# Attention output kept transposed into the mixing stage, with the norm gains moved into w_o and a fourth PSUM bank for turned scores

## The chip, the core and the metric

The kernel is one program on one core of a Trainium2 chip. The metric is device time in microseconds (us) of a run, the median of several. Work is spread over five engines that each run their own instruction stream in order: PE (TensorE: matrix products and transposes), DVE (VectorE), ACT (ScalarE), POOL (GpSimd) and SP (SyncE, which issues DMAs). They meet only at semaphores. A wait written in an engine's stream holds everything that is queued behind it on that engine.

## The reference, cut to what matters

One layer of an encoder runs on 2048 prompt rows and 64 sample rows (2112 rows), model width 1024. All arithmetic is float32.

```python
h = rms_norm(x, g_pre_mix)
q, k, v, logf, gate_b, cu = project(h, w_in, b_f)
o_attn = attn_fn(q, k, v, logf).reshape(b, t, ATTN_DIM)      # 8 heads x 64
o_conv = gate_b * short_conv(cu)                              # 512 channels
merged = jnp.concatenate([rms_norm(o_attn, g_attn_out), rms_norm(o_conv, g_conv_out)], axis=-1)
x = x + rms_norm(merged @ w_o, g_post_mix)
h2 = rms_norm(x, g_pre_mlp)
m = jnp.square(jax.nn.relu(h2 @ w_up)) @ w_down
x = x + rms_norm(m, g_post_mlp)
```

The attention of the sample rows also reads a cache of 512 past keys. `g_attn_out` and `g_conv_out` are gains per channel, so they can stand on either side of the product with `w_o`.

## The kernel before, in words

There are four stages, one after the other: the input projection (`project_inputs`, to about 636 us of the profile), attention (`attend`, to about 1093 us), mixing (`mix_rows`, to about 1310 us) and the MLP (`mlp`). Every float32 product is made from rounded high parts and low rests, as hi\*hi + hi\*lo + lo\*hi, so each operand is split into two parts beforehand.

**Attention.** `attention_order` (L1095) writes one list of steps for two heads, and every engine walks that list four times, each taking the steps that concern it. `queue_of` (L1075) only moves some kinds of step a few places later on ACT and DVE (`DELAY`, L1072). The kinds are: S, a piece of scores (PE L1471 to L1475, DVE L1434); M, the row maximum and the exponentials (DVE L1440, ACT L1389); T, turning a block of exponentials onto its side through PE (L1484, bank `t_bank`) and splitting it (ACT `p_hi` L1393, DVE `p_lo` L1446); V, the product with the values (PE L1500, L1501, bank `o_bank`); O, ACT's copy of the finished `o_bank` to SBUF (`o_t`, L1398); N, the rest of a group; L, the loads of the next head's operands on SP.

A head has five groups of query rows, worked in the order g0 (rows 0 to 511), g4 (the 64 sample rows), g1, g2, g3; their T steps number 4, 2, 8, 12, 16. In `o_t` the 128 partitions hold two halves of 64, one from the high part of the values and one from the rest, that must still be added. N does that in the kernel before: PE turns the four 128x128 blocks into `n_bank` (L1507), ACT copies them (`o_n`, L1404), POOL adds the halves (L1349) and multiplies by the reciprocal of the row sums (L1352), and SP stores the rows to the DRAM tensor `attn` (L1302). N of a group stands after the first two T steps of the group that follows. `att` has five buffers.

L stands at the start of each head. Between the two heads of one list it comes ahead of the N of the first head's g3 (`L ... T T N(g3)`); where the list wraps round, the N of the second head's g3 is the last step of the list and so comes ahead of L. It issues ten DMAs (L93 to L107, about 6 MB), or the eight loads of `w_o` (L1581) in the last head. All of them are issued by SP, which also issues the stores of N.

During the last head POOL splits the eight row blocks of `w_o` into `w_hi` and `w_lo` (`split_weights`, L1599; which blocks after which N is `SPLITS`, L1067), and prepares tile 0 of the mixing stage (L1614 to L1643).

**Mixing.** `mix_rows` works on 17 tiles of rows; tile 0 is the 64 sample rows. For a tile, DVE multiplies the attention rows by the gain (`ag`, L1880), PE turns them (`turn`, L1961), ACT and DVE split them (`a_hi` L1795, `a_lo` L1884); the conv output already lies transposed, and POOL squares and sums it over blocks (L1754 to L1760), multiplies the gain (`cg`, L1763) and makes the rest (`c_lo`, L1766), with `c_hi` from ACT (L1789). The sum of squares over channels is taken by ACT for the attention rows (L1785) and by PE for the conv part (`sum_squares`, L1969), one tile ahead of the products. PE then makes the two products (`multiply`, L1975, banks `a_bank` and `c_bank`, 24 matmuls each). ACT and DVE scale, add, normalise, add x and normalise again (`part` L1822, `mixed` L1900, `scaled` L1908, `x2` L1913, `h2` L1923), and PE turns `h2` (L2025), which ACT copies (L1830). On PE the steady order is: product a of tile t, turn and sum_squares of tile t+1, product c of tile t, turn of h2 of tile t-1. On ACT the front work of tile t+1 begins right behind the copies L1830.

## Time and profile before

| | |
|---|---|
| runs | 2746.72, 2746.88, 2739.39 us; median 2746.72 |
| span of the profiled execution | 2738.8 us |
| own time of the profiled execution | not recorded apart from its span; the median of the runs lies 7.9 us above that span |
| PE busy | 2664.4 us, 97% of the span |
| DVE, ACT, POOL busy | 1520.9, 1126.8, 1308.7 us (56%, 41%, 48%) |
| attention stage | about 636 to 1093 us |
| mixing stage | about 1093 to 1310 us |

The span runs from the first to the last instruction. Busy is the time in which an engine had an instruction in work; PE's ends are modelled, so that its neighbours overlap. In a timeline a line gives the start, the duration, the engine, the source line, the operation and its tiles; "x4" stands for four merged into one. A DMA line on SP gives the time that the issue took on SP, not the transfer.

### The profile page before, as it was taken

How to read it: one execution, taken by the hardware profiler on the slowest of the kernel's cores; microseconds unless marked ns; L12 is line 12 of the kernel's file. 1: busy time of each engine (PE TensorE's matmuls, PEld its weight loads, DVE VectorE, ACT ScalarE, POOL GpSimd, SP SyncE). 2: the span in 40 equal slices, each digit the busy share in tenths (PEclk: the TensorE clock that was granted, in tenths of full speed). 3: DMA queues.
4: the chain of work that ended last, by engine and by line, in shares of the span. 5: the costliest groups of instructions: out<-in, count | busy, mean ns of one | idle time of the engine just before them, and what ended most of it. 6: DMA issues, size and time to landing. Idle time of an engine off the chain costs nothing.

```text
span 2738.8 us, 41595 instructions
## 1 busy us (share of the span) xinstructions
PE 2664.4 (97%) x14966; PEld 2404.3 (88%) x14966; DVE 1520.9 (56%) x2603; ACT 1126.8 (41%) x2099; POOL 1308.7 (48%) x884
## 2 busy tenths in 40 slices
PE   8999999998999999999999999999999999999998
PEld 7899899897887878888899998889999988999996
DVE  5333434247888888666343443665556664556554
ACT  3201301106777877455333332534333344333433
POOL 3233243320110115544476775866556677566664
PEclk9999999999999999999999999999999999999999
DMA  6643544574465543469445456512211272211213
GB/s 196 194 131 102 164 112 138 188 198 123 99 141 132 122 101 113 145 188 252 153 158 176 164 184 218 193 64 74 74 64 61 78 283 94 75 61 63 75 61 108
DMA packets 294353, 364.26 MB, mean 133 GB/s; under 512 B 37576, under 2 KB 245392, under 8 KB 290128
## 3 DMA queue, kind: packets, MB, share of 16 engines
q1 hardware_dynamic: 257152, 316.15, 37.7%
q0 software_dynamic: 11808, 26.74, 3.1%
q10 hardware_dynamic: 25264, 19.66, 2.1%
q8 instruction: 80, 1.31, 0.2%
q14 instruction: 49, 0.40, 0.0%
HBM read 264.30 MB, written 97.94 MB: 132 GB/s over the span
## 4 chain that ended last, share of the span: by engine, by line
PE 45%; POOL 2%; DMA 2%; DVE 1%; issue 1%; ACT 0%; SPq 0%; DVEq 0%; POOLq 0%; ACTq 0%
PE dn_bank L3006 16%; PE up_bank L2982 14%; PE dn_bank L2962 7%; PE up_bank L2937 7%; DMA m_raw_up<-in_w_up 1%; POOL m_y L2517 1%; POOL m_w_up L2466 1%; DMA m_x<-scratch_x 0%; SPq L2342 0%; DVE m_t L2758 0%; DVE m_raw_up L2758 0%; POOL m_u L2509 0%; ACT m_junk L2659 0%; DVE m_y L2863 0%; DVE m_y L2817 0%
## 5 line engine op out<-in xcount | busy, mean ns | idle before, releaser
L3006 PE MATMUL dn_bank<-m_w_dn,m_u 128*128 128x512 f32 x2304 | 528.8, 390 | 0.8 <-DVE m_y L2817 0.5
L3006 PEld LDWEIGHTS dn_bank<-m_w_dn,m_u 128*128 128x128 f32 x2304 | 431.9, 188 | 90.1 <-DVE m_y L2817 0.9
L2982 PE MATMUL up_bank<-m_h,m_w_up 128*128 128x384 f32 x2688 | 476.6, 337 | 9.7 <-DVE m_stage L2772 5.3
L2982 PEld LDWEIGHTS up_bank<-m_h,m_w_up 128*128 128x128 f32 x2688 | 470.6, 189 | 13.7 <-issue 5.8
L2819 DVE TENSOR_TENSOR m_y<-dn_bank,m_y 128x1024 f32<-128x1024 f32 x168 | 205.7, 1224 | 270.4 <-PE dn_bank L3006 270.4
L508 POOL TENSOR_TENSOR w_lo<-w_raw,w_hi 128x1024 fp32r<-128x1024 f32 x72 | 180.9, 2516 | 327.5 <-DVE w_hi L722 327.5
L2509 POOL TENSOR_TENSOR m_u<-m_stage,m_u 128x384 fp32r<-128x384 f32 x128 | 141.5, 1128 | 281.4 <-ACT m_u L2648 281.4
L2466 POOL TENSOR_TENSOR m_w_up<-m_raw_up,m_w_up 128x512 fp32r<-128x512 f32 x128 | 191.8, 1519 | 65.2 <-ACT m_w_up L2616 65.2
L938 PE MATMUL proj<-ha_hi,w_hi 128*128 128x384 f32 (+1 forms) x640 | 212.2, 331 | 0.0
L1446 DVE TENSOR_TENSOR p_lo<-t_bank,p_hi 128x512 fp32r<-128x512 f32 (+1 forms) x336 | 197.9, 599 | 25.2 <-ACT p_hi L1393 24.6
L938 PE MATMUL proj<-ha_hi,w_lo 128*128 128x384 f32 (+1 forms) x640 | 210.0, 328 | 0.0
L938 PE MATMUL proj<-ha_lo,w_hi 128*128 128x384 f32 (+1 forms) x640 | 210.0, 328 | 0.0
L1349 POOL TENSOR_TENSOR att<-o_n 128x256 f32<-128x256 f32 (+1 forms) x40 | 26.2, 654 | 380.1 <-ACT o_n L1404 375.7
L1393 ACT ACTIVATE p_hi<-t_bank 128x512 fp32r<-128x512 f32 (+1 forms) x336 | 171.7, 528 | 65.5 <-PE t_bank L1484 62.5
L2937 PEld LDWEIGHTS up_bank<-m_h,m_up_plain 128*128 128x128 f32 x1440 | 192.4, 188 | 2.5
L2937 PE MATMUL up_bank<-m_h,m_up_plain 128*128 128x256 f32 (+1 forms) x1440 | 193.9, 294 | 0.0
L2648 ACT ACTIVATE m_u<-m_stage 128x384 fp32r<-128x384 f32 x128 | 60.2, 517 | 302.3 <-PE dn_bank L3006 299.6
L2772 DVE TENSOR_TENSOR m_stage<-up_bank,m_stage 128x384 f32<-128x384 f32 x224 | 118.6, 551 | 113.6 <-PE up_bank L2982 107.6
L2616 ACT ACTIVATE m_w_up<-m_raw_up 128x512 fp32r<-128x512 f32 x128 | 76.3, 624 | 242.3 <-PE up_bank L2982 226.4
L2502 POOL TENSOR_TENSOR m_w_dn<-m_raw_dn,m_w_dn 128x2048 fp32r<-128x2048 f32 x32 | 159.4, 4981 | 14.8 <-ACT m_w_dn L2624 14.8
L1500 PE MATMUL o_bank<-p_hi,v_hl 128*128 128x512 f32 (+3 forms) x360 | 139.2, 394 | 8.2 <-DVE p_lo L1446 7.6
L2758 DVE TENSOR_TENSOR m_t<-m_raw_up,m_t 128x512 f32<-128x512 f32 x64 | 145.6, 2276 | 0.0
(304 smaller groups left out, 5674.8 us busy)
## 6 DMA issues: line engine op xcount, KB each, us to landing
m_raw_up<-in_w_up SPq DMA_DIRECT2D x48, 1024.0 KB, 5.4
m_raw_dn<-in_w_down SPq DMA_DIRECT2D x47, 1024.0 KB, 4.9
w_raw<-in_w_in SPq DMA_DIRECT2D x72, 512.0 KB, 4.1
scratch_h_pairs<-m_pieces POOLq DMA_DIRECT2D x12, 1792.0 KB, 8.2
m_h<-scratch_h_pairs SPq DMA_DIRECT2D x14, 1536.0 KB, 11.0
nck<-scratch_ncum SPq DMA_DIRECT2D x8, 1312.0 KB, 18.9
scratch_v_hl<-vhl SPq DMA_DIRECT2D x20, 512.0 KB, 2.7
q_hi<-scratch_q_hi SPq DMA_DIRECT2D x16, 528.0 KB, 7.4
```

What stands on the lines that cost most here:

```text
L508: pool.tensor_tensor(w_lo[:, slot(i)], w_raw[:, i % 2], w_hi[:, slot(i)].bitcast(F32), ALU.subtract).then_inc(w_lo_done, 1)
L938: mm = pe.matmul(out[:, 0:CW[g]], w[:, slot(i), k], h[g][:, k, chunk(g, n)], start=(k == 0 and a == 0), stop=(k == KB - 1 and a == 2))
L1393: act.activation(p_hi[:, x.p, x.cols], t_bank[x.at % T_BANKS][:, x.cols], ACT.Copy).then_inc(hi_done, 1)
L1446: dve.tensor_tensor(p_lo[:, x.p, x.cols], t_bank[x.at % T_BANKS][:, x.cols], p_hi[:, x.p, x.cols].bitcast(F32), ALU.subtract).then_inc(lo_ ...
L2466: pool.tensor_tensor(w_up[:, j, 1], sources[j], w_up[:, j, 0].bitcast(F32), ALU.subtract).then_inc(w_lo_done, 1)
L2502: pool.tensor_tensor(w[:, 1], raw[:, :, :], w[:, 0].bitcast(F32), ALU.subtract).then_inc(dn_lo_done, 1)
L2758: dve.tensor_tensor(to, x, z, op).then_inc(sums_made, 1)
L2819: dve.tensor_tensor(place, bank[:, :], place, ALU.add).then_inc(y_added, 1)
L2937: mm = pe.matmul(up_bank[2 * x + b][:, 0:w], weights[:, b * P:(b + 1) * P], early.rows[2 * x + hp][:, k, :], start=(k == 0 and p == 0), st ...
L2962: mm = pe.matmul(bank[:, cols], u_first[:, x, b, part], w[wp][:, b, cols], start=(b == 0 and p == 0), stop=(b == 1 and p == len(passes) - 1))
L2982: mm = pe.matmul(out, w_up[:, j, wp, k, :], hidden_rows(g, j, hp, k), start=(k == 0 and p == 0), stop=(k == KH - 1 and p == 2))
L3006: mm = pe.matmul(bank[:, cols], part, wd[:, wp, b, cols], start=(b == 0 and p == 0), stop=(b == 1 and p == len(passes) - 1))
```

## The change

It does the following.

- The N step loses PE's turns, ACT's copy `o_n` and the bank `n_bank`. The freed bank becomes a fourth `t_bank`.
- The second half of `o_t` is brought to the partitions of the first by an SBUF to SBUF DMA on SP (`move_rest`, 64 partitions x 512). POOL adds the halves and multiplies by scales that lie along the rows. The scales reach that layout through DRAM: SP stores the reciprocals (`store_scales`, 4-byte elements, at the first T of a group) and loads them back broadcast to 64 partitions (`load_scales`, at the first V). The reciprocal itself moves on DVE from N to the first T.
- `att` has two buffers instead of five, and ACT's copy of `o_bank` for group k waits until the halves of group k-2 are added (`added`).
- SP's stores go to `attn_t`, a transposed DRAM tensor, and are issued at the first T of a later group.
- The gains are multiplied into `w_o` by POOL, one more pass for each of the eight row blocks.
- In the mixing stage the gain products on DVE and POOL, the four turns on PE and ACT's read of `t_bank` go. ACT makes `a_hi`, `c_hi` and the squares of a; POOL makes the squares of c, both rests and the block sums of both; PE sums both with two small products.

The diff, cut to its core:

```diff
-S_BANKS, T_BANKS, O_BANKS = 3, 3, 1
+S_BANKS, T_BANKS, O_BANKS = 3, 4, 1
-A_BUFS = 5
+A_BUFS = 2
...
# SP, attention
+            def store_upto(n):
+                while left[0] < n:
+                    k = left[0]
+                    h, rows = place_of(k)
+                    sp.wait_ge(att_done, k + 1)
+                    sp.dma_start(dr["attn_t"][h * HD:(h + 1) * HD, rows], att[0:HD, k % A_BUFS, 0:rows.stop - rows.start]).then_inc(att_stored[k % A_BUFS], 16)
+                    left[0] += 1
+            def store_scales(it, x):
...
+                sp.wait_ge(recip_done, k + 1)
...
+                    sp.dma_start(dr["rtotal"][h:h + 1, rows].rearrange("o (a p) -> (o p) a", p=P), rtotal[:, m:m + n],
+                                 allow_slow_non_contiguous=True).then_inc(rtotal_stored, 16)
+            def load_scales(it, x):
...
+                sp.wait_ge(rtotal_stored, 16 * (k + 1))
+                if k >= 2:
+                    sp.wait_ge(att_done, k - 1)
+                sp.dma_start(scales[0:HD, k % 2, 0:w], dr["rtotal"][h:h + 1, rows].to_broadcast([HD, w])).then_inc(scales_loaded[k % 2], 16)
+            def move_rest(it, x):
...
+                sp.wait_ge(o_taken, O_BANKS + k + 1)
+                if k >= A_BUFS:
+                    sp.wait_ge(att_stored[k % A_BUFS], 16 * (k // A_BUFS))
+                sp.dma_start(att[0:HD, k % A_BUFS, 0:w], o_t[HD:P, k % 2, 0:w]).then_inc(moved[k % 2], 16)
...
-                if x.kind == "N" and not (x is last_n and it == AGAIN):
-                    store(it, x)
+                if is_first(x):
+                    store_upto(count(it, x) - 1)
+                    store_scales(it, x)
+                if x.kind == "V" and x.first:
+                    load_scales(it, x)
+                if x.kind == "N":
+                    move_rest(it, x)
# POOL, attention
+                pool.wait_ge(moved[k % 2], times(k))
+                pool.tensor_tensor(place, place, o_t[0:HD, k % 2, 0:rows.stop - rows.start], ALU.add).then_inc(added, 1)
+                pool.wait_ge(added, k + 1)
+                pool.wait_ge(scales_loaded[k % 2], times(k))
+                pool.tensor_tensor(place, place, scales[0:HD, k % 2, 0:rows.stop - rows.start], ALU.mult).then_inc(att_done, 1)
# ACT, attention, step O
-                    act.wait_ge(in_rows, upto("O", it, x.at) + 1)
+                    if it or x.at >= 2:
+                        act.wait_ge(added, upto("O", it, x.at) - 1)
# PE, attention
-                elif x.kind == "N" and not (x is last_n and it == AGAIN):
...
-                        mm = pe.transpose(n_bank[:, i * P:(i + 1) * P], o_t[:, x.at % 2, i * P:(i + 1) * P], ident[:, :])
# POOL, w_o
     def split_weights(self, pool, k):
         pool.wait_ge(self.w_loaded[k], 16)
+        pool.wait_ge(self.S["gains_loaded"], 32)
+        pool.tensor_scalar(self.w_raw[:, k, :], self.w_raw[:, k, :], self.gains[:, k:k + 1], None, ALU.mult).then_inc(self.S["w_scaled"], 1)
# POOL, last head
                 if last and x is last_turns[0]:
                     pool.wait_ge(taken, ALL_TAKEN)
                     front.set_ones(pool)
-                    front.conv_first(pool)
-                    front.scale_first(pool)
+                    front.conv_squares(pool, 0, 0)
                 if last and x is last_turns[8]:
-                    front.conv_first_rest(pool)
+                    front.rests(pool, 0, 0)
+                    front.sum_blocks(pool, 0)
# mixing, ACT (first thing of its step for tile t+1)
+        act.activation(self.a_hi[:, s], self.a_in[:, s], ACT.Copy).then_inc(S["a_hi_done"], 1)
...
+        act.activation(self.c_hi[:, s], self.c_in[:, s], ACT.Copy).then_inc(S["c_hi_done"], 1)
...
+        act.activation(self.squares[:, 0], self.a_in[:, s], ACT.Square).then_inc(S["a_squared"], 1)
# mixing, POOL
+        pool.wait_ge(S["a_hi_done"], t + 1)
+        pool.tensor_tensor(self.a_lo[:, s], self.a_in[:, s], self.a_hi[:, s].bitcast(F32), ALU.subtract).then_inc(S["a_lo_done"], 1)
+        pool.wait_ge(S["c_hi_done"], t + 1)
+        pool.tensor_tensor(self.c_lo[:, s], self.c_in[:, s], self.c_hi[:, s].bitcast(F32), ALU.subtract).then_inc(S["c_lo_done"], 1)
...
+        pool.tensor_tensor(q[:, :, 0:2, :], q[:, :, 0:2, :], q[:, :, 2:4, :], ALU.add).then_inc(S["halves_summed"], 1)
...
+        pool.tensor_tensor(self.square_sums[:, :, :], q[:, :, 0, :], q[:, :, 1, :], ALU.add).then_inc(S["blocks_summed"], 1)
# mixing, PE
-            def turn(t, s):
...
             def sum_squares(t):
-                pe.wait_ge(S["csq_one_done"], t + 1)
+                pe.wait_ge(S["blocks_summed"], t + 1)
...
-                pe.matmul(q_bank[:, 0:1], csq_one[:, :], ones[:, :], start=True, stop=True).then_inc(S["c_summed"], 1)
+                pe.matmul(q_bank[:, 0:1], square_sums[:, 0, :], ones[:, :], start=True, stop=True)
+                pe.matmul(q_bank[:, 1:2], square_sums[:, 1, :], ones[:, :], start=True, stop=True).then_inc(S["rows_summed"], 1)
```

## Rows read from the trace of the kernel before

**Rows 1.** Stages by window: us, busy us of PE, PEld, DVE, ACT, POOL, clock, DMA share.
```profile
697.00:754.00 57.00, 53.08 (x344) 45.39 (x343) 46.29 (x148) 44.78 (x85) 6.90 (x12) 1.00 0.43 106
...
1110.00:1295.00 185.00, 185.00 (x920) 154.55 (x919) 125.92 (x204) 95.02 (x207) 86.90 (x77) 1.00 0.71 203
```

**Rows 2.** Groups by line in the attention stage, 640 to 1098 us.
```profile
L1434 DVE CUSTOM_DVE_ANT_0 scores_b<-s_bank,nck 128x512 f32<-128x512 f32 (+2 forms) x188 | 112.0, 619 | 22.8 <-PE s_bank L1472 22.6
...
L1507 PE MATMUL n_bank<-ident,o_t 128*128 128x128 f32 x132 | 21.5, 278 | 7.8 <-ACT o_t L1398 7.8
```

**Rows 3.** Timeline of SP, attention stage: start, us, issue.
```profile
753.28 0.46 SPq L93 DMA_DIRECT2D q_hi<-scratch_q_hi  x1
...
777.71 18.07 SPq L1302 DMA_DIRECT2D scratch_attn<-att  x4
807.63 0.45 SPq L93 DMA_DIRECT2D q_hi<-scratch_q_hi  x1
...
830.74 37.48 SPq L1302 DMA_DIRECT2D scratch_attn<-att  x6
...
1043.12 22.25 SPq L1302 DMA_DIRECT2D scratch_attn<-att  x4
```

**Rows 4.** SP's issue of L102, all heads: ns min/median/max, first and last start.
```profile
L102 SPq DMA_DIRECT2D v_hl<-scratch_v_hl x7: 16952/17257/17646, 636.1 to 988.7; - x7
```

**Rows 5.** Timeline of ACT: the copies of `o_bank`.
```profile
749.33 0.60 ACT L1398 ACTIVATE o_t<-o_bank 128x512 f32<-128x512 f32 x1 [0.20 <-PE o_bank L1501]
...
773.80 0.57 ACT L1398 ACTIVATE o_t<-o_bank 128x512 f32<-128x512 f32 x1
...
807.63 0.60 ACT L1398 ACTIVATE o_t<-o_bank 128x512 f32<-128x512 f32 x1 [0.19 <-PE o_bank L1501]
...
817.32 0.28 ACT L1398 ACTIVATE o_t<-o_bank 128x128 f32<-128x128 f32 x1
...
1047.43 0.28 ACT L1398 ACTIVATE o_t<-o_bank 128x128 f32<-128x128 f32 x1
```

**Rows 6.** DMA: `att` stores by size; L1302 from 830.5 us; L1302 from 1037 us.
```profile
scratch_attn<-att SPq DMA_DIRECT2D x32, 128.0 KB, 2.9
...
DMA to landing us min/median/max: 4.6/4.7/4.8
...
DMA to landing us min/median/max: 1.7/2.7/8.9
```

**Rows 7.** Timeline of POOL, end of attention: splitting one row block of `w_o`.
```profile
1084.95 1.04 POOL L1601 CAST wo_hi<-wo_raw 128x1024 fp32r<-128x1024 f32 x1
1086.07 2.40 POOL L1604 TENSOR_TENSOR wo_lo<-wo_raw,wo_hi 128x1024 fp32r<-128x1024 f32 x1
```

**Rows 8.** Timeline of PE: the first product of the mixing stage.
```profile
1093.38 0.47 PE L1981 MATMUL c_bank<-wo_hi,c_hi 128*128 128x512 f32 x1
```

**Rows 9.** Timeline of PE, a steady tile of the mixing stage.
```profile
1206.18 1.04 PE L2025 MATMUL h_bank<-ident,h 128*128 128x128 f32 x8
...
1212.52 0.60 PE L1966 MATMUL up_bank<-ident,ag 128*128 128x128 f32 x4
1212.95 0.28 PE L1973 MATMUL up_bank<-mix_ones,csq_one 128*128 128x1 f32 x2
1213.09 0.48 PE L1981 MATMUL c_bank<-wo_hi,c_hi 128*128 128x512 f32 x1
```

**Rows 10.** Timelines of ACT, POOL and DVE in that tile, one line each.
```profile
1207.79 0.63 ACT L1785 ACTIVATE junk_a<-a_in 128x512 f32<-128x512 f32 x1
...
1209.11 1.29 POOL L1766 TENSOR_TENSOR c_lo<-cg,c_hi 128x512 fp32r<-128x512 f32 x1 [6.13 <-ACT c_hi L1789]
...
1210.72 1.76 DVE L1908 SCALAR_TENSOR_TENSOR scaled<-mixed,r_m,g_post 128x1024 f32<-128x1024 f32 x1
```

**Rows 11.** POOL's block sums L1756 and L1760: ns min/median/max, times.
```profile
L1756 POOL TENSOR_TENSOR csq<-csq x16: 722/1592/1614, 1100.1 to 1277.8; 128x256 f32<-128x256 f32 x16
...
L1760 POOL TENSOR_TENSOR csq_one<-csq x16: 456/1090/1162, 1100.9 to 1278.6; 128x128 f32<-128x128 f32 x16
```

More of the change, by code:

```diff
@@ L1212, in attend @@
         o_t = sb("o_t", [P, 2, 512])
-        o_n = sb("o_n", [P, 4, 2, HD])
-        att = sb("att", [P, A_BUFS, 4, HD])
+        att = sb("att", [P, A_BUFS, 512])
+        scales = sb("att_scales", [P, 2, 512])
         ident_r, mask_r = pre.ident_r, pre.mask_r
@@ L1276, in attend @@
         o_of = {(x.off, x.g): x.at for x in body if x.kind == "O"}
+        group_at = {at: group for group, at in o_of.items()}
         AGAIN = HEADS // 2 - 1
@@ L1283, in attend, with count, times, place_of @@
         last_turns = [x for x in final if x.kind == "T" and x.off == 1 and x.g == EXTRA - 1]
-        n_of = {(x.off, x.g): x.at for x in final if x.kind == "N"}
         ALL_TAKEN = S_BANKS + per["S"] * (HEADS // 2)
         ALL_SPLIT = T_BANKS + per["T"] * (HEADS // 2)
-        def stored_by(n):
-            return 16 * (per["N"] // A_BUFS * AGAIN + n // A_BUFS + 2)
+        def count(it, x):
+            return upto("O", it, o_of[x.off, x.g])
+        def times(k):
+            return 16 * (k // 2 + 1)
+        def place_of(k):
+            it, n = divmod(k, per["O"])
+            off, g = group_at[n]
+            rows = slice(4 * g * P, 4 * g * P + 4 * P) if g < EXTRA else slice(SEQ, ROWS)
+            return 2 * it + off, rows
+        def is_first(x):
+            return x.kind == "T" and x.blocks[0] == 0
         v_read = {1: 0, 2: per["V"] // 2}
@@ L1293, in _ @@
         def _(sp):
[L1296 to L1303 removed]
+            left = [0]
@@ L1326, in step @@
                 load_values(sp, dr, h, v_hl[x.par], v_loaded[x.par])
+            front.load_gains(sp)
+            loop(sp, "sync", step)
+            store_upto(per["O"] * (HEADS // 2))
             for i in range(A_BUFS):
-                sp.sem_inc(att_stored[i], 16)
-            loop(sp, "sync", step)
-            store(AGAIN, last_n)
-            for i in range(A_BUFS):
-                sp.wait_ge(att_stored[i], 16 * (1 + per["N"] // A_BUFS * (HEADS // 2)))
+                sp.wait_ge(att_stored[i], 16 * (per["O"] // A_BUFS * (HEADS // 2)))
         @block.gpsimd
         def _(pool):
-            pool.sem_inc(added, 1)
             pool.memset(q_hi[1][:, ROWS:].bitcast(F32), 0.0)
```

289 lines of the change are left out of this document (104 added, 185 removed).

## The prediction

> **What bounds the kernel now.** I read the table of stages first, then the groups by line, then the timelines of the engines around one head, around the start of the mixing stage and in one steady tile. All of it is PE's time: in one head of the attention stage PE is busy 53.1 of 57 us beside 46.3 for DVE, and in the mixing stage it never stops (185.0 of 185 us) [rows 1]. The clock is granted in full in both. So work taken from PE is time gained, but only where nothing else becomes the last to arrive. Three places have to be checked: SP's queue, POOL at the end of attention, and the path of the squares in a mixing tile.
>
> SP's queue is the surprise of this profile. At each head SP issues about 6 MB of loads. It begins at 753.28, and the store behind the loads starts only at 777.71, so SP is away for 24.4 us. At the next head it is away from 807.63 to 830.74, 23.1 us [rows 3]. Most of it is one instruction: the issue of a small load of values holds SP for 17.0 to 17.6 us, seven times out of seven [rows 4]. Before, that costs nothing: only stores wait, and five buffers of `att` cover them.
>
> **Part 1, the N step on PE.** 132 turns go. Four turns in a row take 0.43 us of PE's issue (1212.52 to 1212.95 [rows 9]), so 132 are 14.3 us, and 7.8 us of waits in front of them go too [rows 2]: at most 22 us. Below I find that in every head a stretch is paced by SP, not PE; savings inside it are lost, and in g1 and g2 DVE is nearly full. I take a gain of 12, ends 5 and 22. ACT's `o_n` is off the path and counts as nothing. The fourth `t_bank` also counts as nothing: what it can save is a part of the small waits on `p_lo`, covered by the bound.
>
> **Part 2, SP's queue in front of ACT.** After the change ACT's copy of group k waits until POOL has added group k-2, and that needs `move_rest(k-2)`, a DMA on SP. Behind that wait on ACT stand all the following `p_hi` copies, and behind them DVE's `p_lo` and PE's V. Two heads differ.
>
> (a) Between the heads of one list, L comes ahead of the N of g3. ACT copies g3 at 807.63, SP starts L at 807.63 and is back at 830.74. Then come a store (0.4), the store of the scales (0.5) and the copy: 831.6. Stores issued at that place took 4.6 to 4.8 us to land, so they land at 835.5 [rows 3, 6], and a DMA issued behind them hardly earlier. POOL's add is 1.3 (a two-input op over 512 elements took 1.29 [rows 10]): 836.8. The copy of g4, the second group after g3, waits for this add, and took place at 817.32 [rows 5]. Stall 19.5 us, at three heads.
>
> (b) Where the list wraps, the copy of g3's half goes out ahead of L, and L starts a little earlier than before, as the last store is no longer in its way: 749.33 + 0.6 + 0.6 = 750.5; SP is back 24.4 later, 774.9. Store and scales store, 775.8; their landing 4.7, 780.0 to 780.5; `load_scales` waits for exactly that. Load, store, scales store (1.3), then the move of g0 at 781.8, landing 2.9 [rows 6], add 1.3: 786. The copy of g1, at 773.80 [rows 5], waits for the add of g0. Stall 12.1 us, at three heads.
>
> (c) In the last head L is the eight loads of `w_o`; SP is back at 1043.12, but the store behind them took 8.9 us to land [rows 3, 6]. 1043.1 + 0.9 + 8.9 + 1.3 = 1054.2 against the copy of g4 at 1047.43 [rows 5]: 6.8.
>
> Together 3 x 19.5 + 3 x 12.1 + 6.8 = 101.6 us. Something is made up afterwards: during a stall PE and DVE run ahead until DVE's next `p_lo`, which is four pieces of scores at 0.62 on DVE [rows 2], 2.5 us a stall, 17.5 over seven. Net 84. Ends: nothing made up, 102; twice as much (DVE idles 11 us a head [rows 1]), 64.
>
> **Part 3, POOL before the first mixing tile.** Before, PE starts product c of tile 0 at 1093.38 [rows 8], on the heels of the last V. It waits for `c_lo`. POOL's list now, from the add of the last head's g3 half at 1054.2: multiply 1.3; SP's store, scales store and move of g0, 0.9 and 2.9; add and multiply 2.6, which gives 1061.9. Then come two blocks of `w_o`, g4 (0.8), one block, g1 (2.6), three blocks, the squares (1.0), g2 (2.6), two blocks and the two rests (2.6). A block was 1.04 + 2.40 and gaps, 3.5 [rows 7]; the scaling pass has no row. Its ends are the cast (1.04) and the two-input pass (2.40) on as many elements; it has one tensor input like the cast, so I take 1.1 with its gap, 4.6 a block. Sum 9.3 + 0.8 + 4.6 + 2.6 + 13.9 + 1.0 + 2.6 + 9.3 + 2.6 = 46.7, so 1108.6. PE arrives at 1093.4 + 6.8 - 2.5 - 1.5 (its N steps in that head) = 1096.2. Wait 12 us. Ends: 0 if POOL's list begins when it did before, and 12 + 8 x 1.4 = 23 with the dear scaling pass.
>
> **Part 4, a steady mixing tile.** PE loses the turn (0.43) and gains one more product of sums (0.14, from 1212.95 to 1213.09 [rows 9]). But the sums of tile t+1, wanted at 1212.5, now hang on a chain that begins with ACT's copies of h2, released by PE's turn at 1206.18 [rows 9]. ACT is free at 1207.79 [rows 10] and makes `a_hi` (to 1208.4), `c_hi`, the squares of a (to 1209.5). POOL starts `a_lo` at 1208.5, `c_lo` at 1209.75 (1.25 apart for 1.29 ops), the first block add at 1211.0: 512 elements, 1.29, and then 256 elements, 0.72 undisturbed [rows 11]. Undisturbed they end at 1213.1, and PE is late by 0.25 + 0.14 = 0.4 against now. But DVE's `scaled` and `x2` run just then, from 1210.72, or 0.4 later as ACT's squares of `mixed` come later [rows 10]. Beside them POOL's adds took 1.59 and 1.09 us where they take 0.72 and 0.46 alone [rows 11], 2.2 times as much. If both adds pay in full they end at 1215.4: 2.6 us late. The first is partly over before DVE starts and the second outlasts it, so I take 2.0 a tile. Fifteen tiles have such a sum (2 to 16): 30 us, ends 6 and 40.
>
> The Trainium skill (page "SBUF — State Buffer", section "Who interferes with whom") says that a DVE instruction with two SBUF inputs and a GpSimd instruction that reads SBUF exclude each other, the one that starts first holding the port for its whole length. By that, POOL's first add would run to 1212.3 alone, `scaled` behind it (1.76 or less), then the second add, to 1214.8 at the latest: the dear end of this part would be 30 us, not 40. The stretched durations agree that the two disturb each other; that they do so whole instruction by whole instruction no row here says.
>
> **Sum.** -12 + 84 + 12 + 30 = +114 on the execution's span of 2738.8: 2852.8. The median of the runs lies 7.9 above that span, which I keep: 2860.
>
> **Rivals.** *SP is not held* (0.10). If the issue is held by something that the changed order of DMAs avoids, copies land in about 3 us and part 2 is nought. For: the stall in the issue sits on one load of 32 KB alone. Against: it comes in seven heads out of seven with nearly one length [rows 4], and what is issued right behind it still takes 4.7 [rows 6]. Then N gains 17; POOL's list begins 10 us earlier and the wait of part 3 is 7; mixing 30: +20, 2767. The Trainium skill points this way (page "DMA: Bandwidth & Descriptors", section "Issuing engines are not separate DMA queues": issue time is usually small beside the transfer); here one issue of 17 us says otherwise.
>
> *Faster: PE's work decides everywhere* (0.06). It takes both a copy back to POOL in under 9.7 us after the copy of g3 (817.32 less 807.63), and block sums by 1212.5 in a tile, as when the clash with DVE is absent and ACT starts 0.6 earlier. Then -17 for N and 15 x 0.3 = -4.5 in mixing: 2725.
>
> *All at the dear end* (0.06): nothing made up, the scaling pass at 2.40, full clash: -5 + 102 + 23 + 40 = +160, 2907.
>
> **How the numbers follow.** The forecast has 0.75, the three rivals 0.22, and 0.03 lies near no change. Its own range, from its bounds not all met at once, is 2805 to 2900. The range of 8 in 10 also takes in the first rival: 2770 to 2900. A measurement of this kernel can tell 0.3% (8 us) from no change. Slower by more: the forecast, the first and third rival, 0.91; faster 0.06; within 0.3%, 0.03.
>
> **What would show it.** In attention: `o_t` copies of g4 and g1 on ACT with 10 to 20 us of idle before them, released by POOL's `att` add, POOL itself waiting for a DMA, and two different lengths of head; the attention stage some 70 us longer. At the start of mixing: PE waiting some 12 us on POOL's `c_lo`. In a tile: PE waiting about 2 us for POOL ahead of the sums of squares, and a pitch near 14.5 instead of 12.5. I am wrong if ACT's copies show no such idle time: then the order of SP's queue does not matter, and the total falls to that of a rival.

## The result and the profile after

The changed kernel takes 2970.2 us (median of 4 runs, 2965.3 to 2974.8) against 2744.6 of the kernel before (4 runs): 1.081 times as long, 95% interval 1.080 to 1.083. The forecast was 2860, in a range of 2770 to 2900. The sign was right, the size was half of it. The profiled execution's own time is 2970.27 us, its span 2968.7, so 229.9 us over the span before.

First the busy time of each engine in attention, from PE's first product of scores on, and in mixing (as in [rows 1]: stretch, length, busy us of PE, PEld, DVE, ACT, POOL, granted clock, DMA share, GB/s).

```profile
632.10:1262.40 630.30, 453.50 (x2656) 384.54 (x2656) 381.59 (x1195) 345.40 (x651) 113.50 (x92) 0.85 0.43 100
1287.10:1532.00 244.90, 225.19 (x1067) 181.83 (x1068) 128.15 (x181) 109.12 (x220) 124.18 (x92) 0.99 0.60 176
```

The same stretches of the kernel before:

```profile
630.50:1093.40 462.90, 437.74 (x2793) 374.85 (x2793) 381.52 (x1195) 364.18 (x691) 79.78 (x101) 0.99 0.48 119
1093.40:1315.60 222.20, 220.00 (x1104) 184.67 (x1102) 141.77 (x231) 114.67 (x240) 101.54 (x90) 1.00 0.67 193
```

Attention is 167.4 us longer, a gap of 24.7 before mixing is new, mixing is 22.7 longer and the MLP, whose code is the same, 13.5 (1423.2 before, 1436.7 after). With 1.6 us by which attention starts later, that is the whole 229.9.

In attention PE is idle for 176.8 us where it was idle for 25.2, and it is *busier* as well, 453.5 against 437.7, with 132 turns fewer: the mean granted clock fell to 0.85. What it waited for (waits of the changed kernel, 630 to 1330 us: total, times, longest):

```profile
DVE p_lo L1485 <- ACT p_hi L1439: 185.0, 54, 26.2
...
ACT o_t L1445 <- POOL att L1400: 170.9, 8, 28.8
PE o_bank L1534 <- DVE p_lo L1485: 169.9, 25, 25.3
...
PE c_bank L1957 <- POOL c_lo L1671: 24.7, 1, 24.7
```

Read from below it is the chain of the forecast: PE waits for `p_lo`, that for ACT's `p_hi`, and ACT stands at eight copies of `o_t` until POOL has added. ACT's timeline has them in turn, the last head's among them:

```profile
674.66 0.60 ACT L1445 ACTIVATE o_t<-o_bank 128x512 f32<-128x512 f32 x1 [12.40 <-POOL att L1400]
744.90 0.28 ACT L1445 ACTIVATE o_t<-o_bank 128x128 f32<-128x128 f32 x1 [27.07 <-POOL att L1400]
833.12 0.60 ACT L1445 ACTIVATE o_t<-o_bank 128x512 f32<-128x512 f32 x1 [18.99 <-POOL att L1400]
904.40 0.28 ACT L1445 ACTIVATE o_t<-o_bank 128x128 f32<-128x128 f32 x1 [28.80 <-POOL att L1400]
...
1211.92 0.28 ACT L1445 ACTIVATE o_t<-o_bank 128x128 f32<-128x128 f32 x1 [15.12 <-POOL att L1400]
```

Why 27 and 19 where 19.5 and 12.1 were forecast stands on SP's timeline (start, time of the issue), and on POOL's:

```profile
795.92 17.29 SPq L103 DMA_DIRECT2D v_hl<-scratch_v_hl  x1
813.25 0.59 SPq L104 DMA_DIRECT2D v_hl<-scratch_v_hl  x1
813.88 0.52 SPq L1319 DMA_DIRECT2D scratch_attn_t<-att  x1
814.44 0.59 SPq L1330 DMA_DIRECT2D scratch_rtotal<-rtotal  x1
823.37 0.45 SPq L1340 DMA_DIRECT2D att_scales<-scratch_rtotal  x1
...
824.50 0.59 SPq L1328 DMA_DIRECT2D scratch_rtotal<-rtotal  x1
825.20 0.54 SPq L1349 DMA_DIRECT2D att<-o_t  x1
```

```profile
831.77 1.25 POOL L1400 TENSOR_TENSOR att<-att,o_t 64x512 f32<-64x512 f32 x1 [37.00 <-DMA att<-o_t]
```

The 17 us behind the loads are nearly as in [rows 4] (17.3 to 19.3 us over the seven heads). New is the store of the scales, 2 KB in 512 pieces of 4 bytes: issued at 814.44, it has landed at 823.4, since the load behind it waits for exactly that. Over the 32 groups of 512 rows these two issues lie 8.9 us apart (median; 7.7 to 15.4). The store of the 64-row group (L1328, 64 pieces of 4 bytes) follows, and the move issued behind it at 825.20 lets POOL start only at 831.77, 6.6 us later.

POOL at the start of mixing, and a steady mixing tile on PE, POOL and DVE ([rows 7, 9, 10, 11] before):

```profile
1222.42 2.85 POOL L1618 TENSOR_SCALAR wo_raw<-wo_raw,mix_gains 128x1024 f32<-128x1024 f32 x1
1225.33 1.04 POOL L1621 CAST wo_hi<-wo_raw 128x1024 fp32r<-128x1024 f32 x1
1226.46 2.40 POOL L1623 TENSOR_TENSOR wo_lo<-wo_raw,wo_hi 128x1024 fp32r<-128x1024 f32 x1
...
1285.65 1.27 POOL L1671 TENSOR_TENSOR c_lo<-c_in,c_hi 128x512 fp32r<-128x512 f32 x1
...
1416.66 1.30 POOL L1677 TENSOR_TENSOR mix_squares<-mix_squares 128x512 f32<-128x512 f32 x1
1418.04 1.59 POOL L1681 TENSOR_TENSOR mix_square_sums<-mix_squares 128x256 f32<-128x256 f32 x1
```

```profile
1416.81 2.23 DVE L1897 SCALAR_TENSOR_TENSOR scaled<-mixed,r_m,g_post 128x1024 f32<-128x1024 f32 x1
```

```profile
1419.68 0.38 PE L1948 MATMUL up_bank<-mix_ones,mix_square_sums 128*128 128x1 f32 x2 [1.21 <-POOL mix_square_sums L1681]
...
1423.26 0.40 PE L1957 MATMUL c_bank<-wo_lo,c_hi 128*128 128x512 f32 x1
1423.49 0.40 PE L1957 MATMUL c_bank<-wo_hi,c_lo 128*128 128x512 f32 x1
```

The scaling pass takes 2.85 us, and a block 6.4 instead of 4.6. In the tile PE waits 1.21 us, and its products follow one another every 0.233 us; before it was 0.227 in product a and 0.229 in product c.

### The profile page after: what moved, and what is told of

It is laid out like the page before. It is cut to its first block and busy times, and to the rows that moved or that the text cites. A ratio compares the mean times of both kernels' runs of the same rounds, so it can differ in the third digit from the quotient of the medians.

```text
span 2968.7 us, 41220 instructions
## 1 busy us (share of the span) xinstructions
PE 2701.0 (91%) x14796; PEld 2411.4 (81%) x14796; DVE 1510.7 (51%) x2553; ACT 1104.5 (37%) x2042; POOL 1392.6 (47%) x891
## 5 line engine op out<-in xcount | busy, mean ns | idle before, releaser
L2978 PE MATMUL dn_bank<-m_w_dn,m_u 128*128 128x512 f32 x2304 | 542.5, 395 | 1.5 <-POOL m_w_dn L2474 1.5
L2954 PEld LDWEIGHTS up_bank<-m_h,m_w_up 128*128 128x128 f32 x2688 | 469.6, 189 | 12.2 <-issue 5.5
L1534 PE MATMUL o_bank<-p_hi,v_hl 128*128 128x512 f32 (+3 forms) x360 | 147.6, 417 | 170.1 <-DVE p_lo L1485 169.9
L1400 POOL TENSOR_TENSOR att<-att,o_t 64x512 f32<-64x512 f32 (+1 forms) x40 | 43.4, 1084 | 513.1 <-DMA att<-o_t 502.5
L1534 PEld LDWEIGHTS o_bank<-p_hi,v_hl 128*128 128x128 f32 x360 | 70.8, 197 | 190.1 <-DVE p_lo L1485 184.0
L1439 ACT ACTIVATE p_hi<-t_bank 128x512 fp32r<-128x512 f32 (+1 forms) x336 | 170.9, 528 | 81.0 <-PE t_bank L1518 77.0
```

Of the source, the lines that this page charges most:

```text
L1439: act.activation(p_hi[:, x.p, x.cols], t_bank[x.at % T_BANKS][:, x.cols], ACT.Copy).then_inc(hi_done, 1)
L1534: pe.matmul(out, v_hl[par][:, vb, :], p_hi[:, t.p, at], start=x.first and i == 0, stop=False)
L2954: mm = pe.matmul(out, w_up[:, j, wp, k, :], hidden_rows(g, j, hp, k), start=(k == 0 and p == 0), stop=(k == KH - 1 and p == 2))
L2978: mm = pe.matmul(bank[:, cols], part, wd[:, wp, b, cols], start=(b == 0 and p == 0), stop=(b == 1 and p == len(passes) - 1))
```

## The experiments

Each table line is a run; the ratio is to the kernel before beside it, the idle time that of ACT before its `o_t` copies. e1 to e4, e5 to e8, e9 to e12, e13 to e16, and e17 with e18 ran in groups, each group on another chip. A few us between runs of two groups are therefore no finding, unless the intervals of their ratios are apart.

| run | edit | us | ratio (95%) | idle, times |
|---|---|---|---|---|
| e1 | loads spread | 2930.4 | 1.068 (1.065 to 1.070) | 91.4, 19 |
| e2 | 16-byte store | 2915.6 | 1.063 (1.061 to 1.065) | 123.6, 8 |
| e3 | four `o_t` | 2995.2 | 1.092 (1.090 to 1.094) | 146.9, 22 |
| e4 | before, with stalls | 2896.4 | 1.056 (1.054 to 1.058) | |
| e5 | scales loaded late | 2988.6 | 1.090 (1.088 to 1.092) | 179.9, 9 |
| e6 | e1 and e5 | 2936.9 | 1.071 (1.069 to 1.073) | 88.7, 16 |
| e7 | no gain pass | 2983.2 | 1.087 (1.085 to 1.089) | 199.4, 8 |
| e8 | sums behind product c | 3055.2 | 1.115 (1.112 to 1.117) | 197.0, 8 |
| e9 | changed kernel again | 2996.5 | 1.091 (1.089 to 1.094) | 194.3, 9 |
| e10 | gains tile moved | 2982.6 | 1.086 (1.084 to 1.088) | 198.9, 8 |
| e11 | e5 and 16 bytes | 2916.4 | 1.061 (1.059 to 1.063) | 115.6, 9 |
| e12 | e1, e5, 16 bytes, e10 | 2800.2 | 1.019 (1.017 to 1.021) | 8.0, 2 |
| e13 | e12, front earlier | 2772.8 | 1.009 (1.007 to 1.010) | 9.4, 2 |
| e14 | e12, gains on ACT | 2794.7 | 1.017 (1.015 to 1.018) | none |
| e15 | e13 and e14 | 2768.9 | 1.007 (1.006 to 1.009) | none |
| e16 | e15, three `t_bank` | 2769.1 | 1.007 (1.005 to 1.009) | none |
| e17 | e15, last head eased | 2744.0 | 0.998 (0.997 to 0.999) | 2.1, 1 |
| e18 | e17, four `o_t` | 2744.3 | 0.999 (0.998 to 1.000) | none |

### What a stall costs (e4)

```diff
+                    if (x.off, x.g) in ((0, 1), (1, EXTRA)):
...
+                        for n in range(18):
+                            act.wait_ge(idled, left[0])
+                            act.activation(idle[:, :], idle[:, :], ACT.Copy).then_inc(idled, 1)
+                            left[0] += 1
                     act.activation(o_t[:, x.at % 2, 0:width], ...
```

> The kernel before with 18 dummy copies of 128x1024 on ACT ahead of eight O copies, at the places where the changed kernel stalls; some 20 us a place, 160 us in all. If a stall costs its own length less a catch-up of 2.5 us, as forecast, the run takes 2744.6 + 160 - 20 = 2885 us and the granted clock in attention stays above 0.95. If the stalls also lower TensorE's clock, the clock reads 0.82 to 0.90 in attention, the PE products there are longer, and the run takes 20 to 40 us more, 2905 to 2925 us.

The dummies, and the attention stage:

```profile
L1405 ACT ACTIVATE idle<-idle 128x1024 f32<-128x1024 f32 x144 | 152.1, 1056 | 4.4
```

```profile
637.00:1248.70 611.70, 449.09 (x2765) 383.17 (x2765) 380.72 (x1177) 510.84 (x824) 79.62 (x101) 0.89 0.35 89
```

152 us of dummies make attention 155 us longer than before (its window from 637 us: 456.4 us, PE busy 431.3): PE is idle 137.5 us more (162.6 against 25.1), so it makes up some 15, and its unchanged work takes 17.8 us more at a granted clock of 0.89. So the catch-up of the forecast (2.5 us a stall) was near in size, 1.8 a stall, and a price was missing that pays it back: after a stall PE works for a time at 1.2 instead of 2.4 GHz. Behind the stall that ends at 742.79:

```profile
744.00:748.00 4.00, 4.00 (x15) 3.31 (x14) 3.61 (x11) 3.50 (x7) 0.61 (x2) 0.50 0.02 4
...
752.00:756.00 4.00, 4.00 (x26) 3.44 (x25) 2.84 (x12) 2.81 (x7) 0.00 (x0) 1.00 0.00 0
```

The clock reading confirms the second branch, but its 2905 us was too high (the first branch's 2885 too low). In the changed kernel the same account gives 15.8 us more PE time with 132 turns less (14.2 us): 30.0 us. A second reckoning agrees, an estimate that adds up, over slices of 1 us of attention from its first product on, PE's busy time by one less the granted clock: 2.5 us before, 21.2 in e4 and 33.1 in the changed kernel.

### SP's queue (e1, e2, e3, e9, e5, e6, e11, e12)

e1 puts the ten loads of L on a list and issues one at every second T step:

```diff
-                load_queries_keys(sp, dr, h, ...)
+                load_queries_keys(later, dr, h, ...)
...
+                if x.kind == "T" and pending and (it == AGAIN and x.off == 1 or x.at % 2 == 0):
+                    pending.pop(0)()
```

> The loads of a head are issued on SP one at a time, at every second T step, instead of ten in a row; nothing else changes. If SP's stay behind its own loads is what delays the adds, the eight idle times of ACT before its O copies (170.9 us in the changed kernel) fall under 3 us each, the granted clock in attention goes back above 0.95, and the run takes 2765 to 2800 us. If the landing of the small transfers (8 to 10 us each) is what counts, the idle times fall only by the length of the issue that remains covered, under 30 us in all, and the run stays above 2930 us.

e2, and with POOL reading the scales by a stride e11 and e12, store 16-byte pieces:

```diff
-  dr["rtotal"][h:h + 1, rows].rearrange("o (a p) -> (o p) a", p=P)
+  dr["rtotal"][h:h + 1, rows].rearrange("o (p a) -> (o p) a", p=P)
```

> The reciprocals are stored in 16-byte instead of 4-byte pieces, a quarter as many, so that the scales lie in another order than the computation needs; every other instruction is the same. If the 512 pieces of 4 bytes are what makes the round trip of the scales 8 to 9 us, the trip falls to 4 to 5 us, each of the eight idle times of ACT shrinks by about 4 us, and the run is 30 to 40 us shorter than 2970. If the trip is long because of what else is on the queue, the run stays within 8 us of 2970.

e3: `o_t` with four buffers, the wait `added` two groups further back.

> o_t gets four buffers, so that ACT's O copy waits for the add four groups back instead of two. If it is this wait that turns SP's stay into idle time of PE, the idle time before the O copies falls from 170.9 to under 30 us and the run takes 2770 to 2810 us. If another wait stands behind it (the two buffers of att, or POOL's multiply by late scales), about half of the idle time stays, 60 to 100 us, and the run takes 2850 to 2910 us.

e9 is the changed kernel once more. It matters, because it came out 26 us above the first measurement:

> The changed kernel once more, as the reference for the runs beside it. In the second group of runs attention code that is the same as the changed kernel's had 197 and 199 us of idle time before the O copies instead of 171, and every small transfer landed later (10.3 instead of 8.9 us for the same store of scales). If that is the chip and not the code, this run gives the changed kernel's idle time on this chip, anywhere from 165 to 200 us, and a time of 2965 to 3000 us that goes with it. If it gives 171 and 2970 whatever the chip, the second group's difference has to be explained by its edits.

Its 2 KB store of scales and the load behind it lie 9.5 us apart (median of 32) instead of 8.9. In e1, e3, e7, e8 and e10 that distance is 9.7 to 9.9, so e9 is the one to compare the changed kernel's variants with, e1 to e3 too. The kernel before doesn't show such a difference (2741 to 2749). The slower landing was seen on three chips; what it comes from the runs don't tell.

Neither e1 nor e3 did what was expected. In e3 the wait moved: 22 idle times instead of 9, and the same time as e9. In e1 SP is no longer held for 17 us, but the store of `att` that now follows the large load of values holds it for 7.9 to 10.1 us in each of seven heads, and 91 us of idle time stay, in 19 places. The reading of both misses, an argument from the sizes: the forecast had looked at SP's stay behind the loads alone, but the store of the scales takes some 9 us in every group of 512 rows and 6 in the small one. Four times 9 us, 6 and 24 for the loads are more than a head's 57 us [rows 1]. e2 confirms it from the other side. It missed its range of 30 to 40 us by the good side: 55 us under the first measurement, 81 under e9. Its stalls are nearly those of the forecast (19.5 and 12.1 us):

```profile
731.42 0.28 ACT L1445 ACTIVATE o_t<-o_bank 128x128 f32<-128x128 f32 x1 [21.33 <-POOL att L1400]
...
816.54 0.60 ACT L1445 ACTIVATE o_t<-o_bank 128x512 f32<-128x512 f32 x1 [15.28 <-POOL att L1400]
```

With a quarter of the pieces, each four times as large, the distance between store and load is 2.2 us (median of 32) instead of 8.9; 4 to 5 were expected. The number of pieces alone is not the reason: the 64-row group's store, 64 pieces of 4 bytes in every run, took 6.2 to 7.5 us to land in e2, longer than 128 pieces of 16 bytes. It is issued right behind a load and a store, and what that adds was not tried. The Trainium skill (page "DMA: Bandwidth & Descriptors", section "Specifications") puts the least size for full rate at 512 bytes, and says that below it the engines read, change and write back. The runs agree in direction: 2 KB in 4-byte pieces take longer to land than 128 KB of `att` [rows 6]. They also show what that limit does not tell, since 4 and 16 bytes both lie far below it: 8.9 us against 2.2.

Is it SP's standing still, or the store's place in the queue ahead of the move? e5 loads the scales behind the move, so that SP seldom waits for the landing (and counts landed stores on two semaphores instead of one); e6 adds the spread loads; e11 is e5 with 16 bytes; e12 adds all and the gains tile of e10.

```diff
-                if x.kind == "V" and x.first:
-                    load_scales(it, x)
                 if x.kind == "N":
                     move_rest(it, x)
+                    load_scales(it, x)
```

> SP loads the scales of a group behind the move of its half instead of at its first V, so that it no longer stands still for the landing of the store of the scales; the loads of a head stay together. If SP's standing still for that landing is the missing part of the delay, the eight idle times of ACT fall from 170.9 to about 115 us and the run takes 2900 to 2920 us. If the store of the scales holds up the move by its place ahead of it in the queue, whether SP waits or not, the idle times stay within 20 us of 170.9 and the run within 20 us of 2970.

> Both edits together: the head's loads one at a time and the scales loaded behind the move. If SP's two kinds of standing still (behind the loads; for the landing of the scales) are the whole cause, the idle time before the O copies falls under 25 us in all, the granted clock in attention is above 0.95 and the run takes 2760 to 2800 us. If the queue's transfers themselves are the limit (some 8 us for a store of scales, five a head, and 20 us of loads, against a head of 57 us), idle time of 60 us or more stays and the run is above 2860 us.

> The reciprocals are stored in 16-byte pieces and read back with a stride on POOL, so that the result is right, and the scales are loaded behind the move. What is left is SP's stay behind the head's ten loads, as in the forecast. If the forecast's model holds without the slow store, the idle times before the O copies are near 19 and 12 us in turn, 100 to 115 us in all, and the run is 60 to 80 us shorter than e9. If the waits are bound by something else, the idle time stays above 130 us.

> All edits together: 16-byte pieces, scales loaded late, a head's loads spread over its steps, the gains tile moved. If SP's loads and the 4-byte store are the whole cause of the idle time, it falls under 20 us, the granted clock in attention is above 0.95, and the run takes 2755 to 2790 us: attention as long as before, some 10 us of wait for c_lo, 15 x 1.2 us in mixing. If the transfers as such are too much for the queue, idle time of 50 us or more stays and the run is above 2830 us.

e5's ratio is level with e9's (1.090 and 1.091, their intervals overlap), and 180 us of idle time stay: the place in the queue counts, not SP's wait for the scales (second branch). SP now stands ahead of the move instead (818.56 to 826.74 in one head); by the code it waits there for a store of `att` that was issued behind the 4-byte one. e6 keeps 88.7 us, also its second branch: with the loads spread, a 4-byte store lies ahead of every move. e11's 115.6 us are near the forecast's 101.6 with the first head added (4.8 us in it). In e12 the idle time is gone (8.0 us), the clock in attention is back at 0.97, and attention ends at 1097, before at 1093. So there are two causes, the loads in one block and the 4-byte store, and each by itself is enough for stalls: with only one of them gone 89 to 124 us stay (e1, e2, e6, e11), with both gone 8. But e12's total was expected 10 to 45 us shorter. What is left there is outside attention:

```profile
PE c_bank L1976 <- POOL c_lo L1690: 31.3, 1, 31.3
```

### The products that became slower (e10)

```diff
-        self.gains = ctx.enter_context(nc.sbuf_tensor("mix_gains", [P, KB], F32))
...
+        front.gains = sb("mix_gains", [P, KB])
```

> The 32-byte tile of the gains is taken out of the region that lies below all later tiles and put among attention's own tiles, so that the tiles of the mixing stage and the MLP stand at the addresses of the kernel before. Their 128x512 products follow one another every 0.233 us in the changed kernel and every 0.227 in the kernel before. If the shift of all addresses by 32 bytes makes them slow, the pitch goes back to 0.227, mixing and MLP are together 17 to 19 us shorter and so is the run, against e9. If the slower products have another cause (the clock, the order of the work), the pitch stays at 0.233 and the run within 5 us of e9.

The pitch goes back to 0.228, and the MLP takes 1427.9 us against 1435.5 in e9. Over all runs the two sets don't overlap: with the tile where the change put it the MLP takes 1434 to 1439 us (e1 to e3, e5 to e9, e11), with it moved 1423.1 to 1427.9 (e10, e12 to e18), and 1423.2 and 1427.3 in the kernel before and e4, which have no such tile. The run is 13.9 us shorter than e9 where 17 to 19 were expected; 7.6 of them are in the MLP, and the trace does not place the rest. Mixing gained nothing (246.6 against 246.1): the tile stays at 13.9, PE only waits longer (1.3 us), and in two tiles the products then fell to the lower clock for a while:

```profile
1448.18 0.53 PE L1957 MATMUL c_bank<-wo_lo,c_hi 128*128 128x512 f32 x1
1448.51 0.63 PE L1957 MATMUL c_bank<-wo_hi,c_lo 128*128 128x512 f32 x1
1448.94 0.63 PE L1957 MATMUL c_bank<-wo_hi,c_hi 128*128 128x512 f32 x1
```

There they follow every 0.427 us. So the slower products in mixing cost nothing here, those in the MLP 8 us in this pair and 13 between the kernel before and the changed one.

### POOL's list at the start of mixing (e7, e14)

e7 leaves the `tensor_scalar` of L1618 out. e14 does it on ACT, and lets POOL split two blocks a group earlier:

```diff
-        pool.tensor_scalar(self.w_raw[:, k, :], self.w_raw[:, k, :], self.gains[:, k:k + 1], None, ALU.mult)
+        act.activation(self.w_raw[:, k, :], self.w_raw[:, k, :], ACT.Copy, scale=self.gains[:, k:k + 1])
```

> The changed kernel without the pass that multiplies the gains into w_o (the gains are left out of the computation). PE waits 24.7 us for c_lo at the start of the mixing stage and the eight passes are 2.85 us each. If POOL's list is what ends that wait, it falls by 8 x 2.9 = 23 us to 2 us and the run takes 2945 to 2950 us. If the list hangs on the late add of the last head, most of the wait stays and the run is above 2960 us.

> On the kernel of e12: the pass that multiplies the gains into w_o goes from POOL (2.85 us a block) to ACT, and POOL splits its first two blocks one group earlier, in time in which it waited for a transfer. PE waits 31.3 us for c_lo in e12. If POOL's list is what ends that wait, 23 us of it go with the passes and up to 7 with the earlier start: the wait is under 5 us and the run 25 to 32 us shorter than e12. If ACT's eight passes of about 1.1 us hold up p_hi as much, the last V comes 5 to 9 us later and the gain is 18 us or less.

In e7 the wait for `c_lo` is 15.8 us against 25.3 in e9: 8 passes of 2.85 us are gone from POOL, and only 9.5 of the wait, since the list then hangs on the late moves of the last head: between its first block and `c_lo` POOL stands 7.8 and 5.3 us before adds for which it did not wait in the changed kernel. In all e7 is 13.3 us below e9, and their intervals overlap. In e14 it falls from 31.3 to 10.2, but the last O copy comes 15 us later than in e12 (1112.6 against 1097.2), since ACT has eight passes of 1.15 us more and stands 13.0 us before blocks that have not landed:

```profile
1062.90 1.15 ACT L1642 ACTIVATE wo_raw<-wo_raw,mix_gains 128x1024 f32<-128x1024 f32 x1 [5.33 <-DMA wo_raw<-in_w_o]
```

The run is 5.6 us shorter, not clear of the intervals, where 25 to 32 were hoped for: a wait that took the place of another.

### The mixing tile (e8, e13)

e8 swaps `sum_squares(t + 1)` and product c in PE's step. e13 moves `firsts` (now `a_hi` and the squares of a, without `c_hi`) ahead of ACT's copies of h2 (`back_out`), and `c_lo` (`rest_c`, taken out of `rests`) behind POOL's block sums:

```diff
+                if is_tile(t + 2):
+                    front.firsts(act, t + 2, s)
                 if last:
                     back_out(t - 1, 1 - s)
...
                     front.rests(pool, t + 1, 1 - s)
                     front.sum_blocks(pool, t + 1)
+                    front.rest_c(pool, t + 1, 1 - s)
```

> In a mixing tile PE takes the sums of squares of tile t+1 behind product c of tile t instead of ahead of it. If POOL's block sums are late by about 1.5 us a tile there, PE no longer waits for them, the pitch falls from 13.98 to 12.5 to 12.9 us and the run is 15 to 22 us shorter than 2970. If the pitch comes from something else (the clock, DVE's chain), the run stays within 6 us of 2970.

> On the kernel of e12: in the mixing stage ACT makes a_hi and the squares of tile t+2 ahead of its copies of h2 instead of behind them, and POOL makes the block sums ahead of c_lo. In e9, e10 and e12 a tile takes 13.98 us whether PE's products follow every 0.233 or 0.227 us, and PE waits 1.2 or 1.3 us for the block sums. If the sums are late because their squares hang on ACT's turn behind h2, the wait goes, the pitch falls to 12.1 to 12.5 us and the run is 22 to 30 us shorter than e12 (2800). If POOL's stretched passes beside DVE are what makes them late, a wait of 0.5 us or more a tile stays and the run is under 14 us shorter.

e8 was worse by 59 us than e9, where 15 to 22 us less than the changed kernel were expected. The sums, taken 5.6 us later, hold DVE's next step, whose product `h` PE needs, and behind that idle time the clock falls:

```profile
1434.64 1.29 PE L1997 MATMUL h_bank<-ident,h 128*128 128x128 f32 x8 [3.47 <-DVE h L1912]
...
1436.59 0.63 PE L1957 MATMUL a_bank<-wo_hi,a_lo 128*128 128x512 f32 x1
1437.01 0.63 PE L1957 MATMUL a_bank<-wo_hi,a_hi 128*128 128x512 f32 x1
```

e13 hit: 27.4 us shorter than e12, the tile at 12.30 us (12.49 before the change), and no wait ahead of the sums:

```profile
1246.97 0.28 PE L1980 MATMUL up_bank<-mix_ones,mix_square_sums 128*128 128x1 f32 x2
```

So the late sums hung on the place of the front work on ACT and POOL, as part 4 said. e13 moves both engines' work at once, and the sums now end before DVE's `scaled` begins; it does not tell what each move gives, nor part the late start from the clash with DVE. For the clash the changed kernel's trace has the number: the second add took 1.59 us there and 0.73 undisturbed (at 1288.23), 0.86 of PE's 1.21.

### What remains (e15 to e18)

> The edits of e13 and e14 together on e12. If all that made the change slow is then accounted for, the run takes 2738 to 2752 us, level with or just under the kernel before (PE has 132 turns in attention and four a tile in mixing less to do, about 20 us, against what is left of waits and clock in attention). If a part of the loss is still unnamed, it stays above 2760 us.

> e15 with three t_bank instead of four. If the fourth bank is worth nothing, as the forecast took it, the run is within 5 us of e15. If it covers PE's waits for p_lo (24.7 us in attention in e12), the run is 8 us or more longer.

e17 scales the blocks at later T steps, issues the loads of `w_o` by the end of g4 and has `SPLITS = {(0, 3): (4,), (1, 0): (5, 6), (1, QT // 4): (7, 0), (1, 1): (1, 2, 3)}`.

> On the kernel of e15: in the last head ACT scales the blocks of w_o later, when they have landed, instead of standing 13.5 us before them, the loads of w_o are all issued by the end of g4, and POOL splits all eight blocks before the last add of g2. If these two name what is left in the last head, the last O copy comes some 13 us earlier, the wait for c_lo falls from 11.6 to under 6 us, and the run takes 2748 to 2756 us. If the last head is bound by something else, the run is less than 6 us shorter than e15 (2769).

> The kernel of e17 with four buffers of o_t. In e3 four buffers alone gave nothing, since SP's own round of waits was the pace; with that gone, what is left of idle time before the O copies (none in e15, 8 to 9 us in two places in e12 and e13) is all it can take away: 0 to 9 us shorter than e17. If it is longer by more, the wait has only moved to another place.

e15 missed by 17 us; e17 is 25 us shorter, 4 under its own range, and so finds them in the last head, where ACT stood before the weights and POOL's list ended late. e16 is level with e15: the fourth `t_bank` is worth nothing here. e17 brings the last O copy to 1094.8 and the wait for `c_lo` to 4.4 us, and takes 2744.0 us: 4.6 under the kernel before beside it (0.9981, interval 0.9971 to 0.9991), a gain smaller than the 0.3% that counts here as a difference. e18 is level with e17. So e17 has the change with its loss taken out. In it PE still waits 21.9 us for `p_lo` in attention, where before it was 10.1 (7.6 ahead of V and 2.5 ahead of turns) and 7.8 ahead of the turns that are gone:

```profile
PE o_bank L1562 <- DVE p_lo L1513: 21.9, 26, 2.0
```

## Why the forecast was wrong, step by step

| step | forecast | measured |
|---|---|---|
| N on PE | -12 (-22 to -5) | -14.2 of work |
| stalls in attention | 101.6 at 7 places | 170.9 at 8 |
| made up in them | -17.5 | -19.3, of it 7.8 N's own waits |
| lower clock | not in the sum | +30.0 |
| wait for `c_lo` | +12 (0 to 23) | +24.7 |
| mixing tiles | +30 (6 to 40) | +22.7 |
| MLP | not in the sum | +13.5 |
| start of attention | not in the sum | +1.6 |

The measured column adds up to the 229.9 us between the two spans, the forecast's to 114. The forecast then added 7.9 us from span to median; in the changed kernel that distance is 1.5, so the medians lie only 225.6 apart. Of the 116 us that the forecast lacked, 69.3 are in the stalls, 30.0 in the clock, 13.5 in the MLP and 12.7 in the wait for `c_lo`; the other rows take 10 back, most of it in the tiles.

**Part 2** named the right places and the right mechanism, and failed on one sentence: "Stores issued at that place took 4.6 to 4.8 us to land [...] and a DMA issued behind them hardly earlier". It gave the store of the scales the landing time of another store in the same place of the queue [rows 6], though it is 512 pieces of 4 bytes. Each stall came out longer mainly by that (in the first (a) the move issued at 733.52 lets POOL start at 743.55, 10 us later where 4 were counted): the (a) ones 27.1, 28.8 and 28.4 us for 19.5, the (b) ones 19.0, 19.9 and 20.2 for 12.1, (c) 15.1 for 6.8. With 4-byte pieces made 16 (e2) they are 21 and 15. The first head's stall of 12.4 us was overlooked: L stands at the start of that head too. Together 69.3 us, more than half of what the forecast lacked.

**The clock** was in no term. The forecast read 1.00 in [rows 1] and counted a stall as its own length; e4 measured 17.8 us for 152 us of stalls, and in the changed kernel it is 30.0.

**Part 3** had the list right and the pass wrong: "it has one tensor input like the cast, so I take 1.1"; it takes 2.85, outside both ends (1.04 and 2.40). Eight times 1.8 us are 14, and the wait is 24.7 instead of 12. The upper end, 23, was built on the two-input pass and so too low as well.

**Part 4** held. The pitch rose by 1.49 us where 2.0 was forecast; the wait is 1.21, and the slower products, which it did not have, are about 0.25 (24 times 0.006 and 24 times 0.004). Of POOL's two adds only the second was stretched (1.59; the first ran its 1.30), and DVE's `scaled` in their place, 2.23 instead of 1.76 [rows 10]. The Trainium skill (page "SBUF — State Buffer", section "Who interferes with whom") says that the two exclude each other for whole instructions. By that, `scaled`, begun at 1416.81, gets the port when POOL's first add ends, 1417.96, and runs to its end at 1419.04; the second add, begun at 1418.04, waits until then and takes its own 0.73 more, to 1419.8. The trace agrees within 0.2 us: it ends at 1419.63.

**Part 1** was too high, and not for its reasons. With the stalls gone (e17) the 14.2 us of turns are gone from PE too, and attention is still no shorter: 464.1 us from PE's first product at 630.7 to the last O copy, for 462.9 before. PE is idle 4 us more, and the rest went into the clock. By the reckoning in slices 12.6 us are lost to the lower level in e17's attention, 2.5 before. Six times, near the start of a head, PE waits up to 2.0 us for `p_lo` and then works some 3.5 us at the lower level; the kernel before stays at 1.00 from 637 us to the end of attention.

```profile
642.00:644.00 2.00, 0.40 (x4) 0.15 (x2) 1.27 (x7) 2.00 (x6) 0.00 (x0) 1.00 0.98 249
...
646.00:649.00 3.00, 3.00 (x12) 2.69 (x11) 1.77 (x7) 0.12 (x2) 0.00 (x0) 0.50 1.24 220
```

This is likely part of the changed kernel's 30 us as well. Why DVE's `p_lo` comes later there than before, no run shows.

**Small slips** in the sums come to under 2 us: by its own terms (b) is 12.2, the 132 turns are 14.2, and the 0.25 of part 4 is 0.15.

**Rivals.** That SP is not held: refuted, L103 holds it for 17.3 to 19.3 us as L102 did before. That PE's work decides everywhere: not in the changed kernel, but its two conditions are what e13 and e15 to e17 restored together; the best of them (e17) gave 2744 and not 2725, since N's gain is spent on the clock and on waits. The dear end (2907) came closest, but by luck and not by its terms: it had nothing made up and a full clash in the tiles, and neither happened.

## What to carry to other kernels

A transfer made of tiny pieces is priced by their number and size, not by its bytes or by a neighbour's landing time, and everything issued behind it on its queue pays for it too. When a change makes a bounding engine wait, charge the stall and then the slow stretch after it, and read the granted clock in a stretch that already has stalls. Here even waits of 2 us were followed by such stretches, and they took back what the removed work had saved. Before moving a wait out of the way, count all that its engine does in a period: SP's queue was held up by two things, and with either one gone about half of the stalls stayed.

## What the runs showed of the hardware

- A tile of 32 bytes put below the others moved all later SBUF addresses by 32 bytes and made 128x512 products of mixing follow every 0.233 instead of 0.227 to 0.229 us; in the MLP, 8 us (e9 and e10) to 13. Which operand's address it is was not tried, and 384-wide products did not change (337 ns mean in both).
- POOL's multiply by one scalar per partition takes 2.85 us for 1024 elements, longer than its two-input subtraction (2.40), and the same on ACT 1.15.
- A store of 2 KB in 512 pieces of 4 bytes let the load behind it go after 8.9 us (median), in other runs 9.5 to 9.9; 128 pieces of 16 bytes took 2.2 (e2), and 64 pieces of 4 bytes 6.4, in e2 6.7.
- With the loads of a head spread out (e1), the instruction issued behind the large load of values still held SP's issue for 7.9 to 10.1 us.
- Of TensorE's two levels the lower one (1.2 GHz) was seen behind idle time inside mixing tiles too: in e8, where PE was idle 3.5 us a tile, and in two tiles of e10, where it was idle 1.3 as in its other tiles. There 128x512 products follow every 0.427 us. In the changed kernel's steady tiles, with 1.2 us idle, it was not.
